# Eight squared tiles and who adds them: moving three additions from GpSimd to VectorE in a one-core decoder layer

## The chip, the cores and the metric

One core of a Trainium2 chip runs the whole layer in one launch. The core has TensorE (PE; its weight loads are PEld), VectorE (DVE), ScalarE (ACT), GpSimd (POOL) and SyncE (SP), which here only issues DMAs. The metric is the device time of one execution in microseconds.

## What is computed

One hybrid decoder layer on 1024 tokens of width 1024, all float32. Two attention branches, their gated sum and a squared-ReLU MLP come first. The change lies between the MLP and the gate of the per-layer embedding. That part of the reference is:

```python
h = h + jnp.square(jax.nn.relu(n2 @ w_ff1[i])) @ w_ff2[i]
n3 = _rmsnorm(h, g_ple[i])           # y = h * rsqrt(mean(h*h) + EPS) * g
h = h + jax.nn.sigmoid(n3 @ w_ple_gate[i]) * (p[i] @ w_ple[i])
return _rmsnorm(h, g_final)
```

For `n3` the squares of `h` have to be summed over the width for every token.

## The kernel before

The residual `h` is held with the width on the partitions: eight tiles `h[0..7]` of 128 x 1024, one for each 128 features. Every float32 matmul is made of three: each operand is split into a high part (rounded by ScalarE) and a low part (full minus high), and hi*hi, hi*lo and lo*hi are added in PSUM. For weights, ScalarE makes `w_hi` (line 1213) and GpSimd `w_lo` (`lo_parts`, line 1058), slab by slab. A slab is 128 x 1024, two of them make one column group, and there are two buffers.

The second MLP matmul is done as 16 pairs of seven products in Strassen's manner, in an order written out by hand (`SECONDS`, positions `POS_2`). Each product has two halves, `ab` 0 and 1, of six matmuls each. After each half VectorE adds the PSUM bank to a half tile of `h` (`add_product`, line 2172). The last pair ends with P6, P5, P7, P4, P3. P6, P7 and P4 write the same two banks, so that a half of P4 may start only when VectorE has added the same half of P7, a rule that TensorE keeps with `pe.wait_ge(added, ...)`.

Around these last products the preparation of `n3` is woven in, tile by tile in the order `N2_ORDER = [1, 3, 0, 2, 5, 7, 4, 6]`. The code numbers the tiles of this order n = 0 to 7:

- ScalarE: `h_high(n)` (line 1610, in the profile `n_hi<-h,cols`) is the high part of h times the gain, and `h_square(n)` (line 1604) writes the square of a tile to `h_squares[n % 2]`, two buffers. Its queue is high 0, square 0, high 1, square 1, the slab w_hi (the first of w_ple_gate), high 2, square 2, high 3, square 3, high 4 to 7, squares 4 and 5, the second slab w_hi, squares 6 and 7. A square waits until the square two before it has been added in: squares 2 and 3 wait for the first addition, and square n from 4 on waits for the addition of square n - 2.
- VectorE: `h_low(n)` (line 2010, in the profile `n_lo<-h,cols,n_hi`) is the low part. h_low 0 to 3 stand behind the additions of P6, P5, P7 and P4, and h_low 4 to 7 behind those of P3. The additions of squares 4 to 7 (line 2203) follow, each into `sq_sum_2`.
- GpSimd: adds squares 0 and 1 (line 1182), makes the low part of the first slab, adds square 2 and square 3 (line 1187), and then makes the low part of the second slab.
- TensorE: after P3 it starts the gate matmul on the unscaled tiles, `product(...)` at line 2299. The first slab serves n = 0 to 3 and the second n = 4 to 7. After the fifth tile of the eight it runs `square_sums` (line 2680): a matmul with ones over `sq_sum_2`, which needs all eight squares, and then it goes on with tiles 5 to 7.
- From that sum ScalarE makes the root (line 1638) and VectorE its reciprocal (line 2003). `take_gate(0)` (line 2214) scales the finished group with it.

The counter `sq_ready` carries the order of the additions; `SQ3` is its value before the first of these seven.

Of the kernel before, what the change touches and what calls it, by code (L numbers as in the profile page):

```python
# [27 lines left out]
ALU = mybir.AluOpType  # L28
# [70 lines left out]
def build(nc, x, p, positions, g_mix, w_in, g_cq, w_uq, g_ckv, w_ukv, w_pa, w_pb, w_out, g_mlp, w_ff1, w_ff2,  # L99
          g_ple, w_ple_gate, w_ple, g_final, out):  # L100
    _, S, D = x.shape
    FF = w_ff1.shape[2]
    QL, KVL, PL = w_uq.shape[1], w_ukv.shape[1], w_ple.shape[1]
# [14 lines left out]
    OUT_N = D // (2 * WCOL)  # L118
# [17 lines left out]
    with ctx:  # L136
# [3 lines left out]
        def at(name, off, shape, dt=F32):  # L140
            return nc.alloc_sbuf_tensor_at(name, [P] + shape, dt, offset=base + off)
# [38 lines left out]
        ka_hi, ka_lo = at("ka_hi", R2 + 18 * K, [KV_HEADS_A, S], F32R), at("ka_lo", R2 + 34 * K, [KV_HEADS_A, S], F32R)  # L180
        QA_PLACES = [(R2 + 26 * K, R2 + 30 * K), (NX + 24 * K, NX + 28 * K), (T, T + 4 * K), (R1, R1 + 4 * K)]
        qa_raw = [at(f"qa_raw{g}", lo, [YT, 2, P]) for g, (lo, _) in enumerate(QA_PLACES)]
        qa_lo = [at(f"qa_lo{g}", lo, [YT, 2, P], F32R) for g, (lo, _) in enumerate(QA_PLACES)]
        qa_hi = [at(f"qa_hi{g}", hi, [YT, 2, P], F32R) for g, (_, hi) in enumerate(QA_PLACES)]
        gmix_row = at("gmix_row", R2, [D])
# [49 lines left out]
        h_squares = [at(f"h_squares{b}", o * K, [S]) for b, o in enumerate((152, 172))]  # L235
        sq_sum_2 = at("sq_sum_2", 136 * K, [S])
# [52 lines left out]
        def sem(name):  # L289
            return ctx.enter_context(nc.semaphore(name))  # L290
# [78 lines left out]
        h_sq = sem("h_sq")  # L369
        sq_ready = sem("sq_ready")  # L370
# [74 lines left out]
        SQ3 = 2 * OUT_N + 1  # L445
# [51 lines left out]
        PAIRS_2 = 2 * FFN  # L497
# [7 lines left out]
        POS_2 = {key: o for o, key in enumerate(SECONDS)}  # L505
# [8 lines left out]
        def pair_bank(w, name, ab):  # L514
            other = 4 * (1 - EVEN)
            if name == "P2":
                return bank(other + 1 + 2 * ab)
            if name in ("P5", "P3"):
                return bank(other + 2 * ab)
            return bank(4 * EVEN + 2 * (w % 2) + ab)  # L520
# [519 lines left out]
        def _(pool):  # L1040
# [12 lines left out]
            def lo_parts(k):  # L1053
                for _ in range(k):
                    s, first, num, _ = at_.slab()

                    pool.wait_ge(hi_ready, num + 1)
                    pool.tensor_tensor(lo_of(first)[:, :, :], w_raw[s][:, :, :], hi_of(first)[:, :, :].bitcast(F32),  # L1058
                                       ALU.subtract).then_inc(lo_ready, 1)
# [118 lines left out]
                elif w < PAIRS_2 - 1 and name == "P3":  # L1178
                    pair_sum(w + 1, 4)

            pool.wait_ge(h_sq, 2 * OUT_N + 2)
            pool.tensor_tensor(sq_sum_2[:, :], h_squares[0][:, :], h_squares[1][:, :], ALU.add).then_inc(sq_ready, 1)
            lo_parts(1)
            for k in range(2):
                pool.wait_ge(h_sq, 2 * OUT_N + 3 + k)
                pool.wait_ge(sq_ready, SQ3 + 1 + k)
                pool.tensor_tensor(sq_sum_2[:, :], sq_sum_2[:, :], h_squares[k][:, :], ALU.add).then_inc(sq_ready, 1)
            lo_parts(6 * OUT_N - 1)


# [490 lines left out]
        def _(dve):  # L1681
# [319 lines left out]
            def inverse(n):  # L2001
                dve.wait_ge(root_done, n)
                link(dve.reciprocal(rms[:, :], rms[:, :]))
# [3 lines left out]
            def h_low(n):  # L2007
                k = N2_ORDER[n]
                dve.wait_ge(norm_hi, n + 1)
                dve.scalar_tensor_tensor(n2_lo[k][:, :], h[k][:, :], g_ple_c[:, k:k + 1],  # L2010
                                         n2_hi[k][:, :].bitcast(F32), ALU.mult, ALU.subtract).then_inc(norm_lo, 1)
# [105 lines left out]
            def hid_low(i, k):  # L2117
                b = REFILL[k][0]
                for j in range(2):
                    r = 2 * (i % 2) + j  # L2120
                    dve.wait_ge(hid_hi_done, 14 * i + 2 * k + j + 1)
                    dve.tensor_tensor(b_lo[r][:, b, :], b_lo[r][:, b, :].bitcast(F32), b_hi[r][:, b, :].bitcast(F32),  # L2122
                                      ALU.subtract).then_inc(hid_lo_done, 1)
# [37 lines left out]
            def add_product(o, ab):  # L2161
                w, name = SECONDS[o]
                q = 2 * (w % 2) + ab
                k = 2 * q + (name in ("P5", "P7", "P4"))
                part = first if name in ("P1", "P2", "P4") else second
                if w < 2:
                    dve.wait_ge(h_in[2 * (q // 2) + k % 2], 32)
                dve.wait_ge(p_done, 2 * o + ab + 1)
                if (k, part.start) in latest:
                    dve.wait_ge(added, latest[k, part.start])  # L2170
                latest[k, part.start] = add_count(w, name, ab)
                dve.tensor_tensor(h[k][:, part], h[k][:, part], pair_bank(w, name, ab), ALU.add).then_inc(added, 1)  # L2172

            def late_sum(j):
                if j == 0:
                    dve.wait_ge(late_in, 32)
                else:
                    dve.wait_ge(late_done, j)
                out, a, b = ((late_t3[:, :], late_high[:, second], late_low[:, second]),
                             (late_low[:, second], late_low[:, second], late_low[:, first]),  # L2180
                             (late_low[:, first], late_high[:, second], late_low[:, second]),
                             (late_high[:, first], late_high[:, first], late_low[:, first]))[j]
                dve.tensor_tensor(out, a, b, ALU.subtract).then_inc(late_done, 1)

            for o, (w, name) in enumerate(SECONDS):
                add_product(o, 0)
                add_product(o, 1)
                if o == 0:
                    hid_low(0, 4)
                if o in (2, 4):  # L2190
                    hid_low(0, 4 + o // 2)
                if o in LATE_AT:
                    late_sum(LATE_AT.index(o))
                if o - 1 in HIGH_AT:
                    hid_low(*HIGH_AT[o - 1])
                if POS_2[PAIRS_2 - 1, "P6"] <= o < LAST_2 - 1:
                    h_low(o - POS_2[PAIRS_2 - 1, "P6"])
            for n in range(4, 8):
                h_low(n)
            for n in range(4, 8):  # L2200
                dve.wait_ge(h_sq, 2 * OUT_N + n + 1)
                dve.wait_ge(sq_ready, SQ3 + n - 1)
                dve.tensor_tensor(sq_sum_2[:, :], sq_sum_2[:, :], h_squares[n % 2][:, :], ALU.add).then_inc(sq_ready, 1)
            inverse(3)

            def take_gate(q):
# [629 lines left out]
```

## Time and profile before

| what | value |
| --- | --- |
| median of 3 runs | 1603.19 us (1602.77 to 1603.57) |
| the profiled execution's own time | 1601.97 us |
| span of that execution, first to last instruction | 1600.2 us |
| TensorE busy in the span | 1564.4 us (98%) |
| VectorE busy | 1174.3 us (73%) |
| GpSimd busy | 645.2 us (40%) |
| mean granted TensorE clock | 0.997 |

Times inside the trace count from the span's start. The part around the change lies at 1454 to 1496 us. In a timeline the bracket behind a row is the idle time before it and who ended it. Rows with xN are N instructions merged, which follow each other without a wait that shows. In the profile `sq_sum` is also the name shown for `sq_sum_2`, and `n_hi`, `n_lo` stand for `n2_hi`, `n2_lo`.

### The profile page before, as it was taken

How to read it: one execution, taken by the hardware profiler on the slowest of the kernel's cores; microseconds unless marked ns; L12 is line 12 of the kernel's file. 1: busy time of each engine (PE TensorE's matmuls, PEld its weight loads, DVE VectorE, ACT ScalarE, POOL GpSimd, SP SyncE). 2: the span in 40 equal slices, each digit the busy share in tenths (PEclk: the TensorE clock that was granted, in tenths of full speed). 3: DMA queues.
4: the chain of work that ended last, by engine and by line, in shares of the span. 5: the costliest groups of instructions: out<-in, count | busy, mean ns of one | idle time of the engine just before them, and what ended most of it. 6: DMA issues, size and time to landing. Idle time of an engine off the chain costs nothing.

```text
span 1600.2 us, 22709 instructions
## 1 busy us (share of the span) xinstructions
PE 1564.4 (98%) x8512; PEld 1282.0 (80%) x8512; DVE 1174.3 (73%) x1695; ACT 680.0 (42%) x1127; POOL 645.2 (40%) x401
## 2 busy tenths in 40 slices
PE   7999999999999999999999999999999999999997
PEld 5778888788788878788887888888778888888786
DVE  7679999991766676544347777777799999998444
ACT  5432432322576668511335343343444444445223
POOL 2222542122210112022116445444789898885230
PEclk9999999999999999999999999999999999999999
DMA  5311222324400001124442454445595444421112
GB/s 169 96 40 54 93 91 92 92 90 112 118 2 2 28 15 54 54 85 165 131 140 71 145 172 145 150 158 164 210 336 187 145 145 172 161 102 40 47 59 106
DMA packets 115241, 177.47 MB, mean 111 GB/s; under 512 B 19105, under 2 KB 73377, under 8 KB 115009
## 3 DMA queue, kind: packets, MB, share of 16 engines
q1 hardware_dynamic: 111296, 162.44, 31.0%
q10 hardware_dynamic: 3680, 13.63, 2.4%
q8 instruction: 65, 1.06, 0.3%
q14 instruction: 40, 0.32, 0.1%
q0 software_dynamic: 160, 0.02, 0.0%
HBM read 123.24 MB, written 49.68 MB: 108 GB/s over the span
## 4 chain that ended last, share of the span: by engine, by line
PE 91%; DVE 6%; ACT 1%; DMA 1%; issue 1%; POOL 0%; SPq 0%; ACTq 0%; DVEq 0%
PE ps L2299 36%; PE ps L2745 18%; PE ps L2704 16%; PE ps L2574 4%; PE ps L2589 4%; PE ps L2536 2%; PE ps L2558 2%; PE ps L2444 2%; PE ps L2348 1%; PE ps L2383 1%; PE ps L2540 1%; PE ps L2405 1%; PE ps L2506 1%; DMA x_tok<-in_x_dram 1%; DVE b_lo L2122 1%
## 5 line engine op out<-in xcount | busy, mean ns | idle before, releaser
L1058 POOL TENSOR_TENSOR w_lo<-w_raw,w_hi 128x1024 fp32r<-128x1024 f32 x67 | 165.8, 2476 | 486.2 <-ACT w_hi L1213 465.8
L1132 POOL TENSOR_TENSOR a_lo<-s_raw,a_hi 128x512 fp32r<-128x512 f32 x128 | 189.6, 1489 | 95.8 <-ACT a_hi L1497 95.2
L1213 ACT ACTIVATE w_hi<-w_raw 128x1024 fp32r<-128x1024 f32 x67 | 70.9, 1059 | 345.6 <-PE ps L2299 282.5
L2704 PE MATMUL ps<-b_hi,a_hi 128*128 128x512 f32 x448 | 175.3, 391 | 4.2 <-POOL a_lo L1132 1.8
L2745 PE MATMUL ps<-b_hi,a_hi 128*128 128x512 f32 x448 | 174.4, 389 | 2.4 <-DVE h L2172 2.4
L1132 POOL TENSOR_TENSOR a_lo<-f_raw,a_hi 128x512 fp32r<-128x512 f32 x96 | 136.1, 1433 | 96.5 <-ACT a_hi L1497 96.5
L2704 PE MATMUL ps<-b_hi,a_lo 128*128 128x512 f32 x448 | 174.4, 389 | 0.0
L2745 PE MATMUL ps<-b_hi,a_lo 128*128 128x512 f32 x448 | 174.3, 389 | 0.0
L2704 PE MATMUL ps<-b_lo,a_hi 128*128 128x512 f32 x448 | 174.3, 389 | 0.0
L2745 PE MATMUL ps<-b_lo,a_hi 128*128 128x512 f32 x448 | 174.3, 389 | 0.0
L2299 PE MATMUL ps<-n_hi,w_hi 128*128 128x512 f32 x544 | 168.2, 391 | 2.4 <-ACT rel L1273 1.2
L1799 DVE TENSOR_SCALAR_CACHE_REDUCE tested<-sc,bar_i 128x384 bf16<-128x384 f32 (+2 forms) x192 | 169.0, 943 | 1.7 <-POOL sc L1074 0.6
L2299 PE MATMUL ps<-n_hi,w_lo 128*128 128x512 f32 x544 | 167.6, 389 | 0.0
L2299 PE MATMUL ps<-n_lo,w_hi 128*128 128x512 f32 x544 | 167.5, 389 | 0.0
L2172 DVE TENSOR_TENSOR h<-h,ps 128x512 f32<-128x512 f32 x224 | 142.8, 677 | 22.6 <-PE ps L2745 22.0
L2122 DVE TENSOR_TENSOR b_lo<-b_lo,b_hi 128x512 fp32r<-128x512 f32 x112 | 144.1, 1326 | 0.1
L2299 PEld LDWEIGHTS ps<-n_hi,w_hi 128*128 128x128 f32 x544 | 101.8, 188 | 25.2 <-ACT rel L1273 1.7
L2299 PEld LDWEIGHTS ps<-n_hi,w_lo 128*128 128x128 f32 x544 | 102.1, 188 | 21.4
L2299 PEld LDWEIGHTS ps<-n_lo,w_hi 128*128 128x128 f32 x544 | 102.1, 188 | 21.2
L1497 ACT ACTIVATE a_hi<-s_raw 128x512 fp32r<-128x512 f32 x128 | 78.7, 627 | 93.3 <-PE ps L2745 91.7
L2704 PEld LDWEIGHTS ps<-b_hi,a_hi 128*128 128x128 f32 x448 | 84.1, 188 | 23.9 <-POOL a_lo L1132 3.3
L2745 PEld LDWEIGHTS ps<-b_hi,a_hi 128*128 128x128 f32 x448 | 84.1, 188 | 20.8 <-issue 3.2
(354 smaller groups left out, 3112.1 us busy)
## 6 DMA issues: line engine op xcount, KB each, us to landing
f_raw<-in_w_ff_dram SPq DMA_DIRECT2D x64, 512.0 KB, 4.3
b_lo<-hid_scratch SPq DMA_DIRECT2D x112, 256.0 KB, 5.6
hid_scratch<-c_out SPq DMA_DIRECT2D x32, 512.0 KB, 3.7
w_raw<-in_w_in_dram SPq DMA_DIRECT2D x28, 512.0 KB, 3.7
hid_scratch<-t_out SPq DMA_DIRECT2D x15, 768.0 KB, 6.1
gates_scratch<-stage ACTq DMA_DIRECT2D x16, 512.0 KB, 3.5
sig_ab<-gates_scratch SPq DMA_DIRECT2D x8, 1024.0 KB, 5.9
x_tok<-in_x_dram SPq DMA_DIRECT2D x8, 512.0 KB, 10.1
```

The costliest lines, as they stand in the source:

```text
L1058: pool.tensor_tensor(lo_of(first)[:, :, :], w_raw[s][:, :, :], hi_of(first)[:, :, :].bitcast(F32), ALU.subtract).then_inc(lo_ready, 1)
L1132: pool.tensor_tensor(slot(a_lo, o), first_of(o), slot(a_hi, o).bitcast(F32), ALU.subtract).then_inc(a_lo_done, 1)
L1213: act.activation(hi_of(first)[:, :, :], w_raw[s][:, :, :], ACT.Copy).then_inc(hi_ready, 1)
L1497: act.activation(slot(a_hi, o), first_of(o), ACT.Copy).then_inc(a_hi_done, 1)
L1799: ins = dve.tensor_scalar(tested[:, at0:at0 + KEYS[i]], s_i, bar_f[:, f:f + 1], None, ALU.is_ge, ALU.add, accum_out=count_c[:, f:f + 1])
L2122: dve.tensor_tensor(b_lo[r][:, b, :], b_lo[r][:, b, :].bitcast(F32), b_hi[r][:, b, :].bitcast(F32), ALU.subtract).then_inc(hid_lo_done, 1)
L2172: dve.tensor_tensor(h[k][:, part], h[k][:, part], pair_bank(w, name, ab), ALU.add).then_inc(added, 1)
L2299: last = pe.matmul(bank(4 * half + 2 * j + t)[0:w, :], wm, xm[:, t * HALF:(t + 1) * HALF], start=(n == 0 and a and not onto), stop=(n == t ...
L2574: last = pe.transpose(bank(u % RING)[:, k * P:(k + 1) * P], prob_of(n, e)[:, at0:at0 + P], ident[:, :])
L2589: last = pe.matmul(bank(PV_BANK)[e * HEAD_DIM:(e + 1) * HEAD_DIM, a * P:(a + 1) * P], v, prob_t_of(n, e)[:, at0:at0 + P], start=(k == 0), ...
L2704: last = pe.matmul(unit_bank(u, PLACE[name]), w[o % NS][:, j, :], x[j][:, b, :], start=name in ("P1", "P2", "P5") and j == 0 and a, stop=j ...
L2745: last = pe.matmul(pair_bank(w, name, ab), x[(LAST + o) % NS][:, 2 * j + ab, :], y[r][:, b, :], start=name in ("P1", "P2", "P5") and j == ...
```

## The change

The three additions leave GpSimd. In that place GpSimd only makes the low parts of the slabs. VectorE now makes all seven additions: squares 0 and 1 behind h_low 2 (at P7), square 2 behind h_low 3 (at P4), square 3 behind h_low 4, and squares 4 to 7 after h_low 7 as before. The code of ScalarE and TensorE, and all counts of `sq_ready`, stay.

```diff
-            pool.wait_ge(h_sq, 2 * OUT_N + 2)
-            pool.tensor_tensor(sq_sum_2[:, :], h_squares[0][:, :], h_squares[1][:, :], ALU.add).then_inc(sq_ready, 1)
             lo_parts(1)
-            for k in range(2):
-                pool.wait_ge(h_sq, 2 * OUT_N + 3 + k)
-                pool.wait_ge(sq_ready, SQ3 + 1 + k)
-                pool.tensor_tensor(sq_sum_2[:, :], sq_sum_2[:, :], h_squares[k][:, :], ALU.add).then_inc(sq_ready, 1)
             lo_parts(6 * OUT_N - 1)
...
+            def add_square(n):
+                dve.wait_ge(h_sq, 2 * OUT_N + n + 1)
+                dve.wait_ge(sq_ready, SQ3 + n - 1)
+                dve.tensor_tensor(sq_sum_2[:, :], sq_sum_2[:, :], h_squares[n % 2][:, :], ALU.add).then_inc(sq_ready, 1)
...
                 if POS_2[PAIRS_2 - 1, "P6"] <= o < LAST_2 - 1:
                     h_low(o - POS_2[PAIRS_2 - 1, "P6"])
+                if o == POS_2[PAIRS_2 - 1, "P7"]:
+                    dve.wait_ge(h_sq, 2 * OUT_N + 2)
+                    dve.tensor_tensor(sq_sum_2[:, :], h_squares[0][:, :], h_squares[1][:, :],
+                                      ALU.add).then_inc(sq_ready, 1)
+                if o == POS_2[PAIRS_2 - 1, "P4"]:
+                    add_square(2)
+
             for n in range(4, 8):
                 h_low(n)
+                if n == 4:
+                    add_square(3)
             for n in range(4, 8):
-                dve.wait_ge(h_sq, 2 * OUT_N + n + 1)
-                dve.wait_ge(sq_ready, SQ3 + n - 1)
-                dve.tensor_tensor(sq_sum_2[:, :], sq_sum_2[:, :], h_squares[n % 2][:, :], ALU.add).then_inc(sq_ready, 1)
+                add_square(n)
             inverse(3)
```

## Rows read from the trace of the kernel before

**Rows 1.** The page: its span, and the chain that ended last by engine.
```profile
span 1600.2 us, 22709 instructions
...
PE 91%; DVE 6%; ACT 1%; DMA 1%; issue 1%; POOL 0%; SPq 0%; ACTq 0%; DVEq 0%
```

**Rows 2.** The chain in order of time, 1440 to 1500 us: start, length, what.
```profile
1469.39 13.60 PE ps L2299 x60
1482.98 1.84 PE ps L2680 x4
1484.82 8.21 PE ps L2299 x36
```

**Rows 3.** Timeline of PE at P4's begin and the sums: start, length, instruction.
```profile
1463.66 0.47 PE L2745 MATMUL ps<-b_hi,a_hi 128*128 128x512 f32 x1 [0.93 <-DVE h L2172]
...
1482.87 1.96 PE L2680 MATMUL ps<-sq_sum,ones 128*128 128x512 f32 x4
```

**Rows 4.** Timeline of VectorE, 1457 to 1495 us.
```profile
1457.94 1.62 DVE L2010 SCALAR_TENSOR_TENSOR n_lo<-h,cols,n_hi 128x1024 fp32r<-128x1024 f32 x1
1459.49 1.27 DVE L2172 TENSOR_TENSOR h<-h,ps 128x512 f32<-128x512 f32 x2
1460.69 2.23 DVE L2010 SCALAR_TENSOR_TENSOR n_lo<-h,cols,n_hi 128x1024 fp32r<-128x1024 f32 x1
1462.84 1.27 DVE L2172 TENSOR_TENSOR h<-h,ps 128x512 f32<-128x512 f32 x2
1464.04 2.21 DVE L2010 SCALAR_TENSOR_TENSOR n_lo<-h,cols,n_hi 128x1024 fp32r<-128x1024 f32 x1
...
1467.37 2.23 DVE L2010 SCALAR_TENSOR_TENSOR n_lo<-h,cols,n_hi 128x1024 fp32r<-128x1024 f32 x1
...
1470.72 4.86 DVE L2010 SCALAR_TENSOR_TENSOR n_lo<-h,cols,n_hi 128x1024 fp32r<-128x1024 f32 x4
1475.50 7.22 DVE L2203 TENSOR_TENSOR sq_sum<-sq_sum,h_squares 128x1024 f32<-128x1024 f32 x4
1486.01 6.55 DVE L2003 RECIPROCAL rms<-rms 128x1024 f32<-128x1024 f32 x1 [3.29 <-ACT rms L1638]
1493.12 2.36 DVE L2214 TENSOR_TENSOR tmp<-ps,rms 128x1024 f32<-128x1024 f32 x2 [0.56 <-PE ps L2299]
```

**Rows 5.** The same timeline, unmerged: the first and the second addition of VectorE.
```profile
1475.50 1.21 DVE L2203 TENSOR_TENSOR sq_sum<-sq_sum,h_squares 128x1024 f32<-128x1024 f32 x1
1476.82 3.24 DVE L2203 TENSOR_TENSOR sq_sum<-sq_sum,h_squares 128x1024 f32<-128x1024 f32 x1
```

**Rows 6.** Timeline of GpSimd, 1456 to 1490 us.
```profile
1456.07 2.42 POOL L1182 TENSOR_TENSOR sq_sum<-h_squares,h_squares 128x1024 f32<-128x1024 f32 x1 [4.83 <-ACT h_squares L1604]
1458.43 3.40 POOL L1058 TENSOR_TENSOR w_lo<-w_raw,w_hi 128x1024 fp32r<-128x1024 f32 x1
1461.80 6.72 POOL L1187 TENSOR_TENSOR sq_sum<-sq_sum,h_squares 128x1024 f32<-128x1024 f32 x2
1475.35 3.63 POOL L1058 TENSOR_TENSOR w_lo<-w_raw,w_hi 128x1024 fp32r<-128x1024 f32 x1 [6.83 <-ACT w_hi L1213]
1487.00 2.40 POOL L1058 TENSOR_TENSOR w_lo<-w_raw,w_hi 128x1024 fp32r<-128x1024 f32 x1 [8.02 <-ACT w_hi L1213]
```

**Rows 7.** Timeline of ScalarE, 1455 to 1476 us.
```profile
1455.89 1.04 ACT L1213 ACTIVATE w_hi<-w_raw 128x1024 fp32r<-128x1024 f32 x1
...
1458.52 1.06 ACT L1604 ACTIVATE h_squares<-h 128x1024 f32<-128x1024 f32 x1 [0.54 <-POOL sq_sum L1182]
1459.48 1.13 ACT L1610 ACTIVATE n_hi<-h,cols 128x1024 fp32r<-128x1024 f32 x1
```

**Rows 8.** Timeline of PE, a stretch of small matmuls and the first wide ones behind it.
```profile
385.67 3.85 PE L2464 MATMUL ps<-ones,rms_c 1*128 1x1 f32 x32
389.45 1.22 PE L2444 MATMUL ps<-cq_hi,w_hi 128*128 128x512 f32 x2
```

**Rows 9.** Windows: busy us (count) of PE, PEld, DVE, ACT, POOL; PEclk; DMA share, GB/s.
```profile
390.00:395.00 5.00, 5.00 (x18) 4.00 (x17) 0.04 (x1) 0.00 (x0) 0.00 (x0) 0.75 0.22 43
```

## The prediction, written before the change was run

> **What bounds the kernel now.** I read the page first. TensorE is nearly the whole chain that ended last [rows 1], so an edit on VectorE and GpSimd counts only where TensorE waits. Next I read the chain in order of time around the sums: after P3 come five tiles of the gate matmul (60 matmuls in 13.60 us, 0.227 each), the sums of squares, and the other three tiles, without a gap [rows 2]. TensorE's own timeline shows two places where it meets VectorE. At the start of P4 it was idle for 0.93 us until an addition to h ended. At the sums it was just in time: the fifth tile's last matmul started one step of 0.227 before 1482.87, where the sums began, and VectorE's last addition ended at 1475.50 + 7.22 = 1482.72, 0.15 us before [rows 3, 4]. So the slack of the squares is about zero. That is the point of this case: any delay of the last addition holds TensorE one for one, and an earlier one gains nothing by itself, since the sums stand at a fixed place in TensorE's queue.
>
> Then I read the three other engines side by side, to see what each instruction waits for. VectorE is busy without a pause from 1457.94 to 1482.72 [rows 4]. Its h_low takes 1.62, 2.23, 2.21 and 2.23 us while GpSimd works, and 4.86 / 4 = 1.22 us afterwards. These are not slower instructions but waits for the other engine's to end: GpSimd's first addition ends at 1458.49 and h_low 0 at 1459.56, 1.07 later; GpSimd's w_lo ends at 1461.83 and h_low 1 at 1462.92, 1.09 later [rows 4, 6]. GpSimd waits in the same way: w_lo ends 2.27 us after h_low 0, and takes 3.40 instead of 2.40 [rows 6]. The addition at 1475.50 took 1.21 us, and the w_lo that GpSimd had begun at 1475.35 ended 2.27 after it; the next addition took 3.24 and ended 1.08 after that w_lo [rows 5, 6]. The additions to h, with one operand in PSUM, pass through: 1.27 us for two beside the running w_lo [rows 4]. So two instructions of these kinds with all operands in SBUF take turns. The Trainium skill, "SBUF — State Buffer", section on the shared port pair, states the same rule (whoever starts first keeps the pair for the whole instruction); here the trace agrees to 0.02 us.
>
> **The change, part by part.** I replay the queues with these durations. An instruction of VectorE starts some 0.07 before the one ahead of it has ended (h_low 0 ends 1459.56, the next row starts 1459.49), so one costs: h_low 1.20, two additions to h 1.20, an addition of squares 1.14, with 0.11 more where it needs the one just before it (1475.50 + 1.21, then 1476.82) [rows 4, 5].
>
> *First slab and the stall before P4.* GpSimd has nothing before w_lo now, which starts when w_hi is done: 1455.89 + 1.04 and a hop of 0.1, 1457.0 [rows 7]. It runs 2.40, to 1459.4, and h_low 0, started at 1457.94, ends 1.08 later at 1460.5 instead of 1459.56: 0.93 us lost. The additions for P5 follow, h_low 1 starts at 1461.62 and takes 1.20 instead of 2.15, as nothing runs on GpSimd: 0.95 won. The addition for P7 then starts at 1462.82; before it was 1462.84 [rows 4]. The stall before P4 stays, and the removed first addition pays for nothing. P4 and P3 end when they did, and the gate matmul starts at 1469.37.
>
> *h_low 2 and the first addition.* h_low 2 now costs 1.20 from 1464.02 (0.95 won). Squares 0 and 1 have long been there, and the first addition runs 1465.2 to 1466.4. The additions for P4 start at 1466.35 and end before 1467.7, which TensorE needs only at 1469.37.
>
> *The new wait.* Square 2 on ScalarE now waits for this addition. It started at 1458.52 and starts at 1466.46. Behind it in ScalarE's queue stands high 3, for which h_low 3 waits: square 2 takes 0.96 to the next start, high 3 takes 1.13 [rows 7], so h_low 3 starts at 1468.6 instead of 1467.55. VectorE stands idle for 1.05 us. High 4 to 7, queued behind square 3, come in time for h_low 4 to 7. h_low 3 itself wins 0.95.
>
> *Squares 2 and 3.* 1.14 us each: square 2 from 1469.80, the additions for P3 from 1470.93, h_low 4 from 1472.13, square 3 from 1473.33, h_low 5, 6, 7 from 1474.46, 1475.66 and 1476.86, the next addition (square 4) at 1478.05.
>
> *The second slab.* High 6 and 7 (from 1471.64), squares 4 and 5 and the second w_hi follow each other on ScalarE, so that w_hi ends at 1476.7, and GpSimd's w_lo starts at 1476.8, where it was 1475.35 [rows 6]. h_low 7 starts 0.1 later. Which of the two gets its turn matters little: if VectorE does, w_lo ends 2.27 after it at 1480.4 and the addition of square 4 at 1481.5; the other way round both end within 0.1 of this. The wait is 2.2 us where it was 2.03 in the row of 3.24. TensorE needs this w_lo at 1469.37 + 4 x 2.72 = 1480.2, so it waits 0.3 us there, which the next wait contains.
>
> *The end.* Squares 5, 6 and 7: 3 x (1.21 + 0.11) after 1481.5 makes 1485.45. Squares 6 and 7 on ScalarE (1.06 after the addition two before) are ready in time, as before.
>
> As a sum: three additions 3 x 1.14 = +3.4; the wait for high 3 +1.05; h_low 2 and 3 alone -1.9; the second slab +0.2; the first slab 0. That is +2.7 us. The last addition ends at 1485.45 instead of 1482.72 and TensorE, with no slack, starts the sums at 1485.6. Behind them nothing gives the time back: the root, the reciprocal and the three tiles move together, the take_gate waited for TensorE's last tile and not for the reciprocal, which ended 0.56 us earlier, and TensorE is the chain from there [rows 2, 4]. No DMA is issued or moved past by the edit; the load into the slab buffer that w_lo frees goes 1.4 us later and its slab is split only after the root, so it is hidden.
>
> **Bounds.** The port wait at the second slab is between 0 and 2.3 us (no overlap, a whole w_lo). An addition costs 1.14 to 1.32. The wait for high 3 is 0 to 1.3. The nearest rows are this kernel's own, so I take the middle values above.
>
> The profiled execution took 1601.97, and gives 1604.7. The median shown lies 1.2 above it, so the forecast for the median is 1605.9 us.
>
> **A rule that speaks the other way.** Both of the first additions exist as rows: 2.42 us on GpSimd, 1.21 on VectorE [rows 5, 6]. The Trainium skill, "GPSIMD Engine Reference", section 4.1, advises VectorE for elementwise work, about twice as fast; the durations agree, and by it this edit would pay. The rows say that the faster engine is the one that is full here.
>
> **Rivals.**
> *A, likeliest, as above:* +1.8 to +3.8, 1605.0 to 1607.0. Chance 0.62.
> *B, not slower or less so:* the port costs less than replayed. If no turn is waited for (the first w_lo lets h_low 0 by, the second falls between), P4's stall goes (-0.95), VectorE is 0.6 earlier, and the second wait of 2.2 goes: the last addition ends at 1482.65, and TensorE gets there by 1482.0. Then the time is as before, 1603.1; with one of the two waits it is 1603.5 to 1605. Against it: five turns in rows 4 to 6 fit to 0.02 us. Chance 0.19.
> *C, clearly slower:* the clock. TensorE would be idle for 2.4 to 2.7 us before the sums. After 3.85 us of matmuls of one column the granted clock of the next stretch fell to 0.75 on the mean, a spell at 1.2 GHz, and two wide matmuls took 1.22 us, where the usual step is 0.227 each [rows 2, 8, 9]. A quarter of 5 us is 1.25, which I take as 1.2 to 1.7. If the gap before the sums does the same, the time is 1605.9 + 1.5 = 1607.4. After the 0.93 before P4 matmuls ran at full pace. It decides from the first matmul after the gap on. Chance 0.13.
> *D, faster:* what the rule has in mind: VectorE takes over the additions in time it won from GpSimd's turns, P4's stall goes and the squares keep up with TensorE: -0.95, 1602.2. It needs the last addition 3.5 us earlier than I find. Chance 0.06.
>
> **Chances and range.** A measurement of this kernel can tell about 0.2% from no change, 3.2 us (1600.0 to 1606.4). A lies inside but for its upper end (0.09), B and D inside, C outside: same 0.75, slower 0.23, faster 0.02. The range reaches down to B's no cost and up to C: 1603.0 to 1607.7. The likeliest case alone is 1605.0 to 1607.0.
>
> **What would show it.** Right: the last addition of squares near 1485.4; gaps of some 2.7 us in TensorE's timeline between 1480 and 1486, a small one at the second slab and most of it at line 2680, released by VectorE's addition; idle time of VectorE of 1 us before h_low 3, released by n_hi; the first h_low at 2.5 us and the second at 1.27; the stall before P4 unchanged; one addition of squares at some 3.4 us beside GpSimd's second w_lo. Wrong: a stall before P4 below 0.5 us, sums that start by 1483.5, or PEclk below 1.00 between 1480 and 1495.

## The result, and the profile after

| | median us | executions | ratio to before (95% interval) |
| --- | --- | --- | --- |
| before | 1602.77 (1602.35 to 1603.90) | 9 | |
| after | 1607.08 (1604.78 to 1608.22) | 9 | 1.0022 (1.0014 to 1.0030) |

The change makes the kernel slower by 4.3 us in the median, 0.22% by the ratio. The profiled execution is the fastest of the nine: 1604.78 us, 2.8 over the 1601.97 of before, which is itself below all nine of that kernel. So two numbers need a cause, 2.8 in the traces and 4.3 in the medians, and the causes are not the same.

First the place where TensorE meets the squares. TensorE's timeline after:

```profile
1463.99 0.47 PE L2751 MATMUL ps<-b_hi,a_hi 128*128 128x512 f32 x1 [0.89 <-DVE h L2166]
1469.51 0.39 PE L2305 MATMUL ps<-n_hi,w_hi 128*128 128x512 f32 x1
1485.87 1.96 PE L2686 MATMUL ps<-sq_sum,ones 128*128 128x512 f32 x4 [2.60 <-DVE sq_sum L2171]
1498.57 0.73 PE L2305 MATMUL ps<-n_hi,w_hi 128*128 128x512 f32 x2 [0.77 <-DVE tmp L2220]
```

The stall before P4 is still there, 0.89 where it was 0.93 [rows 3]. Before the sums there is a new one of 2.60 us, ended by VectorE's addition of squares. The idle time of 0.77 before the second gate group is what it was. VectorE's timeline shows how the squares came late:

```profile
1458.30 2.55 DVE L2004 SCALAR_TENSOR_TENSOR n_lo<-h,cols,n_hi 128x1024 fp32r<-128x1024 f32 x1
1461.97 1.27 DVE L2004 SCALAR_TENSOR_TENSOR n_lo<-h,cols,n_hi 128x1024 fp32r<-128x1024 f32 x1
...
1465.56 1.22 DVE L2199 TENSOR_TENSOR sq_sum<-h_squares,h_squares 128x1024 f32<-128x1024 f32 x1
...
1468.94 1.28 DVE L2004 SCALAR_TENSOR_TENSOR n_lo<-h,cols,n_hi 128x1024 fp32r<-128x1024 f32 x1 [0.97 <-ACT n_hi L1604]
1470.14 1.22 DVE L2171 TENSOR_TENSOR sq_sum<-sq_sum,h_squares 128x1024 f32<-128x1024 f32 x1
...
1473.66 1.22 DVE L2171 TENSOR_TENSOR sq_sum<-sq_sum,h_squares 128x1024 f32<-128x1024 f32 x1
1474.80 5.80 DVE L2004 SCALAR_TENSOR_TENSOR n_lo<-h,cols,n_hi 128x1024 fp32r<-128x1024 f32 x3
1480.53 5.20 DVE L2171 TENSOR_TENSOR sq_sum<-sq_sum,h_squares 128x1024 f32<-128x1024 f32 x4
```

h_low 0 takes 2.55 where it took 1.62, h_low 1 takes 1.27 where it took 2.23 [rows 4]. The three additions stand between the low parts, at 1.22 us each. VectorE is idle for 0.97 before h_low 3, released by the high part. GpSimd and ScalarE:

```profile
1457.37 2.39 POOL L1058 TENSOR_TENSOR w_lo<-w_raw,w_hi 128x1024 fp32r<-128x1024 f32 x1 [5.77 <-ACT w_hi L1207]
1477.11 2.42 POOL L1058 TENSOR_TENSOR w_lo<-w_raw,w_hi 128x1024 fp32r<-128x1024 f32 x1 [17.34 <-ACT w_hi L1207]
```

```profile
1466.80 1.06 ACT L1598 ACTIVATE h_squares<-h 128x1024 f32<-128x1024 f32 x1 [8.47 <-DVE sq_sum L2199]
1467.77 1.14 ACT L1604 ACTIVATE n_hi<-h,cols 128x1024 fp32r<-128x1024 f32 x1
```

ScalarE stands idle for 8.47 us before square 2, until VectorE's first addition ends, and high 3 behind it releases h_low 3.

Executions of one kernel reach this stage up to 1.5 us earlier or later: the first matmul of the gate starts between 1469.11 and 1470.55 in the four traces of the changed kernel. I therefore compare a stretch inside the trace: from the first matmul of the gate (1469.51 above) to the first of the second gate group (1498.57). Before it is 26.31 us, between these two rows:

```profile
1469.22 0.39 PE L2299 MATMUL ps<-n_hi,w_hi 128*128 128x512 f32 x1
1495.53 0.73 PE L2299 MATMUL ps<-n_hi,w_hi 128*128 128x512 f32 x2 [0.77 <-DVE tmp L2214]
```

After it is 29.06. The difference of 2.75 is nearly all of the 2.81 between the two profiled executions. The other 1.5 us of the median are not in this trace.

### The profile page after: what moved, and what is told of

The parts are those of the page before. It is cut to its first block, busy times and chain, and to the rows that moved or that the text cites. A ratio compares the mean times of both kernels' runs of the same rounds, so it can differ in the third digit from the quotient of the medians.

```text
span 1602.9 us, 22709 instructions
## 1 busy us (share of the span) xinstructions
PE 1564.6 (98%) x8512; PEld 1282.1 (80%) x8512; DVE 1176.5 (73%) x1698; ACT 679.7 (42%) x1127; POOL 633.5 (40%) x398
## 4 chain that ended last, share of the span: by engine, by line
PE 89%; DVE 7%; issue 1%; DMA 1%; ACT 1%; POOL 0%; SPq 0%; DVEq 0%; ACTq 0%
PE ps L2305 35%; PE ps L2751 18%; PE ps L2710 16%; PE ps L2580 4%; PE ps L2595 4%; PE ps L2542 2%; PE ps L2564 2%; PE ps L2450 2%; PE ps L2354 1%; PE ps L2389 1%; PE ps L2546 1%; PE ps L2411 1%; PE ps L2512 1%; DMA x_tok<-in_x_dram 1%; DVE b_lo L2116 1%
```

## The experiments

They ran in three groups, each on one chip and beside the kernel before, whose medians were 1602.91 (29 executions), 1603.04 (33) and 1603.27 (16). The table is in the order of these groups: four, four and the last rows. The middle columns are read in each trace: idle time that the trace shows directly before the sums, and the stretch just defined.

| kernel | idle before the sums | stretch | median us | over before |
| --- | --- | --- | --- | --- |
| before | 0 | 26.31 | | |
| again (the change) | 2.59 | 29.03 | 1607.32 | +4.4 |
| high_first | 0.78 | 27.85 | 1603.84 | +0.9 |
| sums_later | 0 | 28.48 | 1605.85 | +2.9 |
| lows_spread | 0.42 | 26.87 | 1602.19 | -0.7 |
| one_more | 1.21 | 27.64 | 1604.61 | +1.6 |
| two_more | 2.66 | 30.73 | 1607.04 | +4.0 |
| first_stays | 1.26 | 27.67 | 1604.36 | +1.3 |
| slab_sooner | 1.12 | 27.57 | 1604.33 | +1.3 |
| look_1, look_2 (the change) | 2.57, 2.57 | 30.65, 30.53 | 1607.40, 1606.33 (one each) | |
| three_more | 3.85 | 32.85 | 1609.39 | +6.1 |
| spread_slab | 0 | 26.42 | 1601.96 | -1.3 |

**again.** No edit.

> The changed kernel once more, in more executions. The first theory (the replay of VectorE's queue) says that the last addition of squares is 2.7 us late and that this is all: nearly every execution at 1604.8 to 1605.9 us, and a gap of 2.6 us before the sums. The second theory says that the gap itself costs TensorE more in most executions (the granted clock falls behind it), and the profiled one was a lucky one: a median near 1607, executions spread over 3 us and more where those of the kernel before lie within 1.5, and the longer ones with the lower mean granted clock.

Measured: 1604.35 to 1607.90 in seven executions, median 1607.32, ratio 1.0028 (1.0017 to 1.0040). The profiled one, 1604.35, is again the fastest. Seen together with the nine of the result, 5 of 16 lie between 1604.3 and 1606.0, and 11 between 1606.6 and 1608.3; the two longest have mean clocks of 0.996 and 0.995, the shortest 0.997. The second theory's median and spread came.

**high_first.** On ScalarE:

```diff
-                    for n in range(2, 4):
-                        h_high(n)
-                        h_square(n)
+                    h_high(2)
+                    h_high(3)
+                    h_square(2)
+                    h_square(3)
```

> The changed kernel with ScalarE's high part 3 placed ahead of square 2, so that h_low 3 doesn't wait for a square that waits for VectorE. The replay says: VectorE's idle 0.97 us before h_low 3 goes, the last addition of squares ends 1.0 us earlier, the gap before the sums shrinks from 2.6 to 1.6 us, and the profiled execution takes 1.0 us less than that of the changed kernel (1603.8 against 1604.8). The rival (the idle time of VectorE was not on the path, since the turns with GpSimd's second w_lo decide the end) says no difference: gap 2.6. If the clock takes part, the median falls by more than the 1.0 us, and the spread shrinks.

Measured: VectorE's idle time before h_low 3 is gone. The stretch is 1.18 us shorter than in again, where 1.0 was expected. The idle time shows in two pieces, 0.30 for the second slab's w_lo and 0.78 for the squares. The median falls by 3.5 us, three times what the trace gives, and the spread shrinks to 1603.4 to 1605.2. So the wait was on the path, and in the median shortening the gap won more than its length.

**sums_later.** On TensorE, in the kernel after:

```diff
-                    after=lambda n: late_sums() if n == KT else None)
+                    after=lambda n: late_sums() if n == KT + 1 else None)
```

> The changed kernel with the matmul of the sums after the sixth tile of the gate matmul instead of the fifth. TensorE gets to it at about 1486.0, when the sums are ready, so the gap of 2.6 us before it goes. If only TensorE's place in its queue costs the time, the kernel is back at the time before (1602.8). The replay says that the chain sums, root, reciprocal, first scaling is what counts: it starts no earlier, so TensorE waits instead for the scaling of the first group (idle there 0.77 before, now about 2.9 us), and the time is 0 to 0.5 us under that of the changed kernel. If a gap of idle time lowers the clock, the executions spread as much as with the changed kernel, since the gap has only moved.

Measured: no idle time before the sums, and 2.98 in front of the second gate group instead:

```profile
1498.48 0.73 PE L2305 MATMUL ps<-n_hi,w_hi 128*128 128x512 f32 x2 [2.98 <-DVE tmp L2220]
```

The stretch is 0.55 shorter than in again. So it isn't TensorE's place in its queue, but the chain from the last square over the root to the first scaling. This trace also holds the clock's part. A window of it, 1500 to 1505 us (busy us and count of PE, PEld, DVE, ACT and POOL, then PEclk, DMA share and GB/s):

```profile
1500.00:1505.00 5.00, 5.00 (x18) 3.98 (x18) 1.50 (x1) 3.47 (x2) 0.00 (x0) 0.74 0.04 15
```

From 1505 on PEclk is 1.00 again. The gap had moved, and the fall of the clock with it, to behind the stretch: from the first matmul of the second gate group to the end of the span this execution takes 106.0 us, the four traces of the changed kernel 104.3 to 104.4. The median is 1.5 under that of again, where at most 0.5 was expected. Six of the eleven executions took 1605.8 or more (mean clock 0.995 to 0.997), five 1604.7 to 1605.4 (all 0.998).

**one_more, two_more, three_more.** The kernel before, with h_low 7, h_low 6 and 7, or h_low 5 to 7 each computed once more on VectorE ahead of the real one. The repeated instruction writes the same values, so it only delays what stands behind it. The edit shown is that of two_more.

```diff
             for n in range(4, 8):
+                if n in (6, 7):
+                    k = N2_ORDER[n]
+                    dve.wait_ge(norm_hi, n + 1)
+                    link(dve.scalar_tensor_tensor(n2_lo[k][:, :], h[k][:, :], g_ple_c[:, k:k + 1],
+                                                  n2_hi[k][:, :].bitcast(F32), ALU.mult, ALU.subtract))
                 h_low(n)
```

> The kernel before, with its three additions on GpSimd, and h_low 7 computed twice on VectorE: a pure delay of about 1.3 us ahead of the additions of squares (1.20 and a wait for its own end), nothing else moved. Both theories: a gap of about 1.3 us before the sums. The replay says 1.3 us over the kernel before. The clock theory says the same here, since the gap is short as that of high_first was: 1.3 (to 1.8 if a few executions lose the clock).

> As one_more, with h_low 6 and h_low 7 each computed twice: a pure delay of about 2.6 us, as long as the gap of the changed kernel, without any of its moves. The replay alone says 2.6 us over the kernel before, and executions as close together as those of before. The clock theory says that the gap of 2.6 us costs what it costs in the changed kernel: two groups of executions, one at +2.0 to +3, the other another 2 to 3 us longer, the median at +4 to +4.7. If only the changed kernel has the second group, something in its moved additions makes it and not the gap.

> As two_more, with h_low 5, 6 and 7 each computed twice: a gap of about 3.9 us in TensorE before the sums. The replay alone says 4.0 us over the kernel before. The clock theory says that nearly every execution now loses the clock: 5.6 us or more over the kernel before, none within 4.0, and a trace with PEclk below 1.00 behind the gap.

Measured, one_more: stretch +1.33, median +1.6, eleven executions between 1603.8 and 1605.2, and a trace with PEclk 1.00 from 1440 to 1580 us. two_more: median +4.0, as with the change, though no addition had moved. Its trace has the gap and then the slow clock:

```profile
1487.33 3.22 PE L2685 MATMUL ps<-sq_sum,ones 128*128 128x512 f32 x4 [2.66 <-DVE sq_sum L2208]
```

The next pair of matmuls takes 1.84. PEclk is 0.79 from 1485 to 1490 and 0.87 from 1490 to 1495. How much of the time is delay can be read from VectorE: from the gate's first matmul to the end of the last addition it is 13.5 us before, 14.8 in one_more, 16.3 in two_more and 17.5 in three_more, that is 1.3, 2.8 and 4.0 more. So of the 4.42 by which two_more's stretch is longer, 2.8 are the delay and 1.6 the clock. The expected two clear groups did not show: ten of eleven lie from 1606.3 to 1607.9, one at 1605.2. three_more: all five executions between 1608.8 and 1609.6, and a stretch of +6.5, of which the delay is 4.0 and the clock 2.6 (PEclk 0.64 from 1485 to 1490, 0.68 from 1490 to 1495). In the medians, one repeated low part costs its own length and 0.3, two cost 1.2 more than theirs, three 2.1 more; the shortest of the five executions of three_more is 1.6 over the delay.

**look_1, look_2.** No edit, one execution each, for a trace of a long one.

> The changed kernel, one execution with its trace. The two traces of it so far (1604.8 and 1604.4 us) show no fall of the clock, while 11 of its 16 timed executions took 1606.6 or more. If those are executions in which the granted clock falls behind the gap, a trace of one of them shows what two_more's shows: PEclk below 1.00 between 1485 and 1495, the four matmuls of the sums at 3.2 instead of 1.96 us, and 1.6 us more from the sums to the second gate group. If a trace of 1606.6 or more shows full clock there, the theory falls.

> The same again: with about 11 in 16, at least one of the two looks should fall into the longer group, with PEclk below 1.00 behind the gap.

Measured: both took over 1606, and both show the slow clock. TensorE in look_1, and its windows (columns as above):

```profile
1486.88 3.29 PE L2686 MATMUL ps<-sq_sum,ones 128*128 128x512 f32 x4 [2.57 <-DVE sq_sum L2171]
1489.19 1.78 PE L2305 MATMUL ps<-n_hi,w_hi 128*128 128x512 f32 x2
```

```profile
1480.00:1485.00 5.00, 4.31 (x20) 3.23 (x18) 4.79 (x4) 1.95 (x2) 0.53 (x1) 1.00 0.34 105
1485.00:1490.00 5.00, 3.12 (x5) 1.34 (x6) 1.63 (x2) 0.17 (x1) 0.00 (x0) 0.74 0.01 3
1490.00:1495.00 5.00, 5.00 (x22) 4.12 (x21) 3.63 (x1) 2.06 (x2) 2.40 (x1) 0.92 0.00 0
```

The same gap as in the profile after (2.57 and 2.60), but the four matmuls of the sums take 3.29 instead of 1.96, the next pair 1.78, and the pairs from 1490.81 on 0.62, the usual pace. The stretch is 30.65, 1.6 more than in the profile after; in look_2 it is 1.5 more, at PEclk 0.66 from 1485 to 1490. The mean clock of a whole execution is too coarse to sort executions by: it is 0.997 in look_2, as in the profile after, which has no slow spell here. The Trainium skill, "TensorE: Matmul & The Clock Gate", Part 1, says that the gate knows two levels, 1.2 and 2.4 GHz; the pairs agree with it: slow ones for a spell, then at once full ones, none between for long. In finer windows of look_1 PEclk is 0.50 throughout from 1487.5 to 1490.5 and 1.00 from 1491 on.

The finer windows also show when the clock falls. In look_1 it is still 1.00 during the whole gap and 0.90 from 1486.8 to 1487.5, so it falls some 0.5 us after the sums have started. In look_2 it is 0.79 from 1485 to 1486 and 0.50 behind that, and the sums start at 1485.92: it has fallen before the gap ends. In three_more it is 0.73 from 1486 to 1486.8 and 0.50 from there on, while the sums start at 1487.93.

**first_stays.** The kernel after, with the addition of squares 0 and 1 back on GpSimd:

```diff
+            pool.wait_ge(h_sq, 2 * OUT_N + 2)
+            pool.tensor_tensor(sq_sum_2[:, :], h_squares[0][:, :], h_squares[1][:, :], ALU.add).then_inc(sq_ready, 1)
             lo_parts(1)
...
-                if o == POS_2[PAIRS_2 - 1, "P7"]:
-                    dve.wait_ge(h_sq, 2 * OUT_N + 2)
-                    dve.tensor_tensor(sq_sum_2[:, :], h_squares[0][:, :], h_squares[1][:, :],
-                                      ALU.add).then_inc(sq_ready, 1)
```

> Half the change: the addition of squares 0 and 1 stays on GpSimd, those of squares 2 and 3 are on VectorE. The replay says: square 2 on ScalarE no longer waits for VectorE (-1.0), one addition less on VectorE (-1.1) and one h_low in GpSimd's shadow as before; the last addition of squares ends 0.9 to 1.6 us later than in the kernel before, the gap is about 1.3 us, the time 1604.0 to 1604.6. A theory by which each addition given to VectorE costs the same third says two thirds of the profiled execution's 2.8: +1.9.

Measured: stretch +1.36, median +1.3, idle 1.26. The expected values came. The first addition alone is half of what the trace of the change shows, since it brings the wait of 0.97 with it; by an equal share for each addition two thirds, +1.9, would be left.

**slab_sooner.** high_first, and on ScalarE:

```diff
+            hi_parts(1)
             for n in range(4, 8):
                 h_high(n)
             h_square(4)
             h_square(5)
-            hi_parts(1)
             h_square(6)
```

> high_first (high part 3 ahead of square 2) and, on ScalarE, the second slab's w_hi ahead of high 4 instead of behind square 5. GpSimd's w_lo then runs from about 1471, mostly beside the additions to h, which take their second operand from PSUM, and VectorE waits for it about 1.1 us instead of 2.2. The replay says: the last addition of squares ends another 1.1 us earlier, no gap before the sums, the time within 0.3 us of the kernel before, with the stall of 0.9 us before P4 still there. If turns between GpSimd and VectorE were not the price, the gap stays at 0.8 as in high_first.

Measured: not so. The stretch is only 0.28 shorter than in high_first, and 1.12 us of idle time stay, about as much as the 0.30 and 0.78 of high_first together. VectorE's timeline says why:

```profile
1472.64 2.50 DVE L2005 SCALAR_TENSOR_TENSOR n_lo<-h,cols,n_hi 128x1024 fp32r<-128x1024 f32 x1 [0.42 <-ACT n_hi L1604]
```

h_low 4 waits 0.42 for its high part, which now stands behind the slab on ScalarE, and then takes 1.23 more than its 1.27, while w_lo runs from 1471.65. Together that is 1.65, where the turn in the kernel before costs 2.03 [rows 5], and that in high_first 2.0 (its last four additions take 7.22 us, here 5.20). The additions to h beside it end at 1472.22, so most of w_lo still lies under h_low 4.

**lows_spread.** The kernel before, with its additions on GpSimd:

```diff
+            LOWS_AT = [POS_2[PAIRS_2 - 2, "P3"]] + [POS_2[PAIRS_2 - 1, name] for name in ("P6", "P7", "P4")]
...
-                if POS_2[PAIRS_2 - 1, "P6"] <= o < LAST_2 - 1:
-                    h_low(o - POS_2[PAIRS_2 - 1, "P6"])
+                if o in LOWS_AT:
+                    h_low(LOWS_AT.index(o))
```

> The kernel before, its three additions on GpSimd, with h_low 0 moved to the additions of the last but one pair's P3, where VectorE pauses 0.67 us between additions to h, h_low 1 at P6, nothing at P5, h_low 2 at P7 and h_low 3 at P4. The replay says: the addition for P7 no longer stands behind an h_low that waits for GpSimd, the stall of 0.93 us before P4 goes, all behind it moves up by 0.9, the last addition of squares too, and the time is 0.9 us under that of the kernel before (1601.9 against 1602.8). The rival is that GpSimd's turns only fall elsewhere and delay the additions for P4, for which the gate matmul waits: no difference, or slower by up to 1 us.

Measured: the stall before P4 is gone, but 0.42 us of idle time appear before the sums, since TensorE comes sooner and the squares don't quite. Over the stretch that costs 0.56 of the 0.93 won. Median 1602.19, 0.7 under before, ratio 0.9997 (0.9988 to 1.0006): the direction is as expected, the interval does not exclude no change.

**spread_slab.** lows_spread with the edit of slab_sooner.

> lows_spread (the kernel before with h_low 0 to 3 spread so that the stall before P4 goes) and the second slab's w_hi ahead of high 4 on ScalarE. lows_spread left a gap of 0.42 us before the sums; in slab_sooner the earlier slab brought the sums forward by 0.28. The replay says 0.3 to 0.5 us under lows_spread: about 1601.9 us, 1.0 under the kernel before. The rival: the slab's w_hi waits for the last product and holds ScalarE's high 4 to 7 behind it, h_low 4 waits for them, and the time is that of lows_spread or up to 0.5 more.

Measured: neither the stall before P4 nor a gap before the sums is left:

```profile
1482.35 1.96 PE L2681 MATMUL ps<-sq_sum,ones 128*128 128x512 f32 x4
1495.03 0.72 PE L2300 MATMUL ps<-n_hi,w_hi 128*128 128x512 f32 x2 [0.77 <-DVE tmp L2215]
```

The median is 1601.96, 1.3 under the 1603.27 of its group and the lowest of all kernels here; ratio 0.9993 (0.9984 to 1.0002). It is the best version, by an amount that this measurement only just fails to tell from none. Beside the changed kernel (1607.1 to 1607.3) it is clear.

## Why the prediction was right, and where it wasn't

**What TensorE waits for: right.** The slack at the sums was zero and the last addition decides. one_more shows it with the additions where they were: 1.3 us more on VectorE are 1.3 us more in the stretch.

**First slab and the stall before P4: right.** h_low 0 at 2.55 (2.56 worked out), h_low 1 at 1.27, the stall 0.89. The removal of GpSimd's first addition wins nothing, since w_lo starts when ScalarE delivers it and holds h_low 0 instead.

**The new wait: right.** 0.97 where 1.05 was worked out. high_first takes away that wait alone and the stretch falls by 1.18.

**The three additions on VectorE: right,** at 1.22 each, 1.14 from start to start. **The second slab: right in size, wrong in who went first.** I had VectorE's h_low 7 ahead; GpSimd's w_lo took its turn (2.42 us, not delayed) and h_low 7 waited, 3.41. As said, it ended the same way, except that TensorE did not wait for that slab, and the long row is h_low 7 and not an addition of squares.

**The sum: right.** +2.7 was predicted, the stretch says 2.75 and 2.72, and the two profiled executions lie 2.8 apart. That the profiled execution came out at 1604.78 against 1604.7 is partly luck: with the same stretch again's took 1604.35, since it reached the stage 0.4 us sooner.

**The median: inside the range, but the step that failed is rival C's chance.** C was priced rightly: 1.2 to 1.7 us, measured 1.6 in look_1, 1.5 in look_2 and 1.6 in two_more. It wrote that the clock decides from the first matmul after the gap on; the fall itself came before that matmul in look_2 and three_more and some 0.5 us behind it in look_1. But I took 0.13 for it and called A without it the likeliest. The changed kernel has now run 18 times: 13 took 1606.3 to 1608.2, 5 took 1604.3 to 1606.0, and the two traces above 1606 show the slow clock, the two below 1605 the full one. The executions between have no trace, and the times pass from one group into the other without a gap, so one or two near 1606 may belong to the other side. So it is the common case, and the median of 1607.08 is C's 1607.4 rather than A's 1605.9. With it falls the share I gave to a difference within 0.2%: the ratios are 1.0022 and 1.0028, on the slower side, though the interval of the first (1.0014 to 1.0030) reaches below 1.002. (By their parts the chances of same and slower add up to 0.76 and 0.22 and not to 0.75 and 0.23, which changes nothing.) Of the signs of being wrong, PEclk below 1.00 between 1480 and 1495 did not show in the profile after, and showed in both longer executions. What misled me was to weigh the gap of 0.93 before P4, after which the clock held, against one stretch of matmuls of one column, after which it fell; no row of before had an idle time of 2 to 3 us in a busy stretch, and I read the lack of a row as a low chance.

**B and D** fell: no turn between GpSimd and VectorE was missing, and the stall before P4 stayed.

**Who starts first: read too strongly.** The prediction has it that whoever starts first keeps the port pair, and that the trace agrees to 0.02 us. What agrees so closely is how long the loser waits: it ends 1.07 to 1.09 us after the winner (VectorE) or 2.27 after (GpSimd). Who wins does not: in its own rows GpSimd's w_lo starts at 1475.35, VectorE's addition at 1475.50, and w_lo is the one that waits [rows 5, 6].

**Open:** why the clock falls in one execution and not in the next. The medians of the two groups of the changed kernel differ by 2.1 us, the traces by 1.5 to 1.6. The arrival at the stage explains how that can be: look_1 took 2.62 more than the profile after, 1.59 of it in the stretch and 1.04 because it reached the gate's first matmul later (1470.55 against 1469.51), and whoever parts executions by time puts the late ones among the slow. Whether some also have a longer spell no trace shows. high_first's median is 0.6 under what its stretch says. In the traces 0.3 of that lies behind the stretch (104.4 us to the end of the span, 104.7 before); the rest I can't assign.

## What to carry to other kernels

Before work moves to a faster engine, replay the queues of all engines around it: here the faster engine was the full one, and an addition at half the price cost 1.1 us each plus a wait of 1 us that ran through a third engine's queue. Where two engines take turns, moving an instruction away wins only if nothing else steps into its turn. And price an idle gap of TensorE twice: its own length, and the matmuls behind it at half clock. Here the second part showed in none of the traces with gaps up to 1.3 us, and by the times in few of their executions; at 2.6 to 2.7 us it came in most, at 3.9 by the times in all five.

## What the runs showed that I had not expected

The fall of the clock differs from execution to execution of one program: after the same gap of 2.57 to 2.60 us it came in two of four traces of the changed kernel. A profile of the fastest execution hides it, so a median that lies above what the trace explains is a reason to take another trace.

The start times do not say who gets the turn when both engines start within 0.2 us of each other. In the kernel after, w_lo started at 1477.11 and h_low 7 0.08 later: w_lo went first, and so it did with 0.08 or 0.09 in five other traces. But w_lo lost with 0.15 in the kernel before and with 0.16 in lows_spread, and in high_first, with 0.07 between them, it lost two turns in a row:

```profile
1476.31 4.75 POOL L1058 TENSOR_TENSOR w_lo<-w_raw,w_hi 128x1024 fp32r<-128x1024 f32 x1 [16.29 <-ACT w_hi L1207]
```

It took 4.75 instead of 2.42, and TensorE waited 0.30 us for it.
